# A second DMA queue for part of the expert weights: the down matrices' transfers issued by ScalarE

## The reference

```python
D_MODEL = 1024; SEQ = 256; N_EXPERTS = 16; CAPACITY_FACTOR = 2; EXPERT_FF = 2 * D_MODEL
# expert_w_gate_2, expert_w_up_2: (1, 16, 1024, 2048)   expert_w_down_2: (1, 16, 2048, 1024)
# every expert chooses capacity = 2 * 256 / 16 = 32 tokens by their affinity;
# for its 32 tokens it computes  (silu(x @ w_gate) * (x @ w_up)) @ w_down,
# and the results, scaled by the affinity, are added to those tokens' rows of h
```

## Time and profile before

| | us |
|---|---|
| median of three runs | 1963.32 (1962.98 to 1967.84) |
| the profiled execution, its own time | 1964.53 |
| its span in the trace | 1962.7 |
| busy time: TensorE matmuls | 1537.9 (78%) |
| busy time: VectorE | 622.9 (32%) |
| busy time: ScalarE | 525.6 (27%) |
| expert weight transfers issued | 192, of 2048 KB each |
| median from issue to landing, gate, up, down | 46.9, 45.9, 45.2 |

### The profile page before, as it was taken

The page is one execution under the profiler, slowest core; times in us unless marked ns, Lnnn a source line. Parts: engine busy times, 40 slices in busy tenths (PEclk is TensorE's granted clock), DMA queues, the critical chain, the costliest instruction groups (busy, mean ns, idle before and its releaser), DMA issues.

```text
span 1962.7 us, 25924 instructions
## 1 busy us (share of the span) xinstructions
PE 1537.9 (78%) x11225; PEld 1047.0 (53%) x11243; DVE 622.9 (32%) x956; ACT 525.6 (27%) x859; POOL 134.1 (7%) x151
## 2 busy tenths in 40 slices
PE   7999999999999997899898656666556666665655
PEld 7888999897999897689573211121111221111111
DVE  4565444666444544445742000000000000000000
ACT  6445343545434445435531000000000000000000
POOL 0251000030000013310200000000000000000000
PEclk9999999999999989999989877677887777778787
DMA  9443555443555444223186999999999999999997
GB/s 272 135 143 124 185 192 182 140 142 117 184 181 191 121 127 129 65 68 108 45 341 278 428 427 428 428 427 428 428 427 427 428 427 427 428 427 428 428 428 309
DMA packets 138529, 542.00 MB, mean 276 GB/s; under 512 B 10062, under 2 KB 103459, under 8 KB 113859
## 3 DMA queue, kind: packets, MB, share of 16 engines
q1 hardware_dynamic: 138386, 540.50, 70.1%
q0 software_dynamic: 48, 0.13, 0.0%
HBM read 539.56 MB, written 1.05 MB: 275 GB/s over the span
## 4 chain that ended last, share of the span: by engine, by line
PE 48%; DMA 40%; DVE 5%; ACT 3%; POOL 2%; issue 1%; SPq 0%; DVEq 0%; ACTq 0%; POOLq 0%
DMA ew<-in_expert_w_down_dram 21%; PE bank L1039 12%; PE bank L1040 11%; PE bank L1041 11%; DMA ew<-in_expert_w_up_dram 9%; DMA ew<-in_expert_w_gate_dram 9%; PE bank L1518 3%; PE bank L1534 2%; POOL arena L663 1%; PE bank L1178 1%; PE bank L1061 1%; ACT wH L706 1%; PE bank L1123 1%; PE bank L1252 1%; PE bank L1046 1%
## 5 line engine op out<-in xcount | busy, mean ns | idle before, releaser
L1518 PE MATMUL bank<-ew,xeT 128*32 128x512 f32 x2048 | 334.1, 795 | 184.1 <-DMA ew<-in_expert_w_up_dram 130.8
L1555 DVE TENSOR_TENSOR wL<-ring,wH 128x2048 fp32r<-128x2048 f32 x128 | 294.8, 2303 | 285.2 <-ACT wH L706 284.9
L706 ACT ACTIVATE wH<-ring 128x2048 fp32r<-128x2048 f32 x128 | 244.1, 1907 | 308.8 <-PE bank L1041 306.7
L1039 PE MATMUL bank<-xH,wH 128*128 128x256 f32 x1056 | 302.7, 287 | 4.4 <-DVE wL L1555 4.2
L1040 PE MATMUL bank<-xL,wH 128*128 128x256 f32 x1056 | 299.4, 284 | 0.0
L1041 PE MATMUL bank<-xH,wL 128*128 128x256 f32 x1056 | 299.4, 283 | 0.0
L1518 PEld LDWEIGHTS bank<-ew,xeT 128*32 128x32 f32 x2048 | 66.8, 132 | 435.3 <-DMA ew<-in_expert_w_up_dram 210.7
L1534 PE MATMUL bank<-ew,tok 128*32 128x256 f32 x2048 | 178.9, 511 | 100.1 <-DMA ew<-in_expert_w_down_dram 93.2
L1039 PEld LDWEIGHTS bank<-xH,wH 128*128 128x128 f32 x1056 | 203.0, 192 | 10.4 <-issue 8.1
L1040 PEld LDWEIGHTS bank<-xL,wH 128*128 128x128 f32 x1056 | 203.1, 192 | 0.8
L1041 PEld LDWEIGHTS bank<-xH,wL 128*128 128x128 f32 x1056 | 203.1, 192 | 0.0
(11 more groups left out here) (274 smaller groups left out, 1803.2 us busy)
## 6 DMA issues: line engine op xcount, KB each, us to landing
ew<-in_expert_w_gate_dram SPq DMA_DIRECT2D x64, 2048.0 KB, 46.9
ew<-in_expert_w_up_dram SPq DMA_DIRECT2D x64, 2048.0 KB, 45.9
ew<-in_expert_w_down_dram SPq DMA_DIRECT2D x64, 2048.0 KB, 45.2
ring<-in_w_gate_up_dram SPq DMA_DIRECT2D x44, 1024.0 KB, 5.1
ring<-in_w_down_dram SPq DMA_DIRECT2D x22, 1024.0 KB, 4.9
ring<-in_w_in_dram SPq DMA_DIRECT2D x22, 1024.0 KB, 5.3
ring<-in_w_out_dram SPq DMA_DIRECT2D x12, 1024.0 KB, 4.9
ring<-in_w_in_fox_dram SPq DMA_DIRECT2D x10, 1024.0 KB, 8.8
```

The costliest lines, as they stand in the source:

```text
L706: act.activation(wH[:, n % 2, w], ring[:, slot(n), w], ACT.Copy).then_inc(w_hi, 1)
L1039: pe.matmul(out, lh, rh, start=start, stop=False)
L1518: mm = pe.matmul(bank[half][32 * j:32 * j + 32, :], xeT[:, k, CAP * e:CAP * e + CAP], w_[:, m, 512 * j:512 * j + 512], start=(k == 0), sto ...
L1555: dve.tensor_tensor(wL[:, n % 2, w], ring[:, slot(n), w], wH[:, n % 2, w].bitcast(F32), ALU.subtract).then_inc(w_split, 1)
```

## The change

The function that issues one unit, `load_expert`, moves out of SyncE's block and takes the issuing engine as an argument. The first expert is left as it was. From the second expert on, SyncE leaves out units 8 to 11. ScalarE issues these four one behind the other, between its wait for the gate product (`e_used` at 12 e + 4) and its Silu. A slot's earlier unit has then been multiplied in every case, since the latest that unit 11 needs is `e_used` at 12 e + 2. The slots, the sizes and the order in which TensorE uses the units stay the same.

```diff
+        def load_expert(queue, e, u):
+            g = e * EU + u
+            if u < 8:
+                src = (e_gate, e_up)[u // 4][0, e].rearrange("(u p m) f -> u p (m f)", p=P, m=2)[u % 4]
+            else:
+                src = e_down[0, e].rearrange("(u p m) d -> u p (m d)", p=P, m=4)[u - 8]
+            queue.dma_start(ew[:, eslot(g), :], src).then_inc(e_full[eslot(g)], 16)
...
             for g in range(ESLOTS, NE * EU):
-                sp.wait_ge(e_used, g - ESLOTS + 1)
-                load_expert(g // EU, g % EU)
+                if g % EU < 8 or g < EU:
+                    sp.wait_ge(e_used, g - ESLOTS + 1)
+                    load_expert(sp, g // EU, g % EU)
...
                 act.wait_ge(e_used, e * EU + 4)
+                if e > 0:
+                    for u in range(8, EU):
+                        load_expert(act, e, u)
                 act.activation(sg, bank[0][:, :], ACT.Silu).then_inc(e_sg, 1)
```

More of the change, by code:

```diff
@@ L554, in _ @@
                 load_rows(n, w_out2[0], 2 * P * i)
[L556 to L562, removed]
             dif = att_base["dif"]
@@ L566, in _ @@
             for g in range(3):
-                load_expert(0, g)
+                load_expert(sp, 0, g)
             sp.wait_ge(w_split, NU - 4)
-            load_expert(0, 3)
+            load_expert(sp, 0, 3)
             sp.wait_ge(sn_ss, 4)
             sp.wait_ge(mTL, 4)
-            load_expert(0, 4)
+            load_expert(sp, 0, 4)
             sp.wait_ge(w_split, NU)
-            load_expert(0, 5)
-            load_expert(0, 6)
+            load_expert(sp, 0, 5)
+            load_expert(sp, 0, 6)
             sp.wait_ge(w_used, NU)
-            load_expert(0, 7)
-            load_expert(0, 8)
+            load_expert(sp, 0, 7)
+            load_expert(sp, 0, 8)
             sp.wait_ge(xe_mm, KD)
-            load_expert(0, 9)
+            load_expert(sp, 0, 9)
             for g in range(ESLOTS, NE * EU):
-                sp.wait_ge(e_used, g - ESLOTS + 1)
-                load_expert(g // EU, g % EU)
+                if g % EU < 8 or g < EU:
+                    sp.wait_ge(e_used, g - ESLOTS + 1)
+                    load_expert(sp, g // EU, g % EU)
             for q in range(4):
```

## The result

The changed kernel took 2007.97 us (median, 2006.18 to 2010.9) beside 1964.63 us of the kernel before in the same session: a ratio of 1.022, 95% interval 1.020 to 1.024. The prediction was 1969.3 us with a range from 1961 to 1988; it was wrong. The profiled execution has a span of 2009.1 us, 46.4 more than before. (Of the many executions of the kernel before that stand beside the experiments, one took 2501 us; it counts in no ratio.)

What follows compares the result with a forecast made beforehand. The prediction took the sixteen DMA engines to bound the expert stage, 58.8 us per expert. SyncE 0, Silu 0, cycle 0 and end +6 on a median of 1963.3 gave 1969.3 us, range 1961 to 1988.

Steps and rivals of the forecast that it cites:

- what bounds the kernel, and what a change could touch: Expert stage: DMA engines set the pace, 58.8 us per expert; only idle engines or work behind the last landing move time.
- Silu: ScalarE: Silu waits behind four issues, 1.3 us, at worst 11.6, but this is hidden; counted as 0.
- the order of service: DMA engines with two full queues: taken as half and half, packet by packet.
- SyncE in part: SyncE without the down units: skipping four issues per expert is worth nothing, gate units issued no earlier; counted as 0.
- The bound of 2.9 us for one issue: ScalarE's issues: 0.33 us each, up to 2.9 when the queue is full, so at worst 11.6 us for four.
- service in the order of issue: Rival on the two queues: down units land behind units issued earlier, end unchanged, +0, 1963 us; chance 0.12.
- the cycle costs nothing: Expert stage, steady state: engines never stop, since the down-unit path takes 57.5 us against the engines' 58.8; counted as 0.
- The path by the down units: From one complete gate product to the next through down-unit landings and products: 57.5 us, 1.3 us to spare.
- settles at three units of backlog: Expert cycle: about three up units outstanding at each complete gate product, unit 7 landing 29.1 us behind it.
- The forecast's median of 40 us: Down units in the steady state: median time from issue to landing falls to 40 us.
- the cycle is longer: Rival: expert cycle exceeds 58.8 us; at 61, about 1985 us; costlier half, about 2075 at share 0.4; chance 0.2.
- the end, +6: Last expert: TensorE ends 8 to 10 us after the last landing, before 3.1; 5.2 to 7 later, taken as 6.

Runs made afterwards that it cites:

- experiment 7: Changed kernel with ScalarE's Silu placed ahead of its four down-unit issues instead of behind them: 2005.99 us, ratio 1.022 to the kernel before.
- experiment 8: Changed kernel with the next expert's gate units 0 and 1 held on SyncE's queue for four more products: 1963.68 us beside 1963.56 of the kernel before.
- experiment 1: Changed kernel's late down-unit moments (e_used = 12 e + 4), but all transfers issued by SyncE on one queue: 1961.47 us beside 1965.06 of the kernel before.
- experiment 3: Changed kernel with TensorE multiplying zeros while it waits, from the second expert on, no transfer touched: 1973.56 us, ratio 1.005 to the kernel before.
- experiment 5: Changed kernel with TensorE multiplying zeros in its waits, but not between the last expert's down units: 1966.22 us beside 1963.95 of the kernel before.
- experiment 2: Changed kernel with ScalarE's four issues two gate units earlier, at e_used = 12 e + 2: 1965.12 us beside 1965.06 of the kernel before.
- experiment 9: Changed kernel with ScalarE issuing the down units near the moments of the kernel before: 1975.9 us beside 1963.56 of the kernel before.
- experiment 6: Changed kernel with ScalarE's four issues one gate unit earlier, at e_used = 12 e + 3: 1974.67 us beside 1963.56 of the kernel before.

## Why the prediction was wrong, step by step

**Right: what bounds the kernel, and what a change could touch.** Only idle engines or work behind the last landing could move the time; the whole loss is idle engines: 951.3 less 905.8 us is 45.5, against 46.4 in the span. The rest is the start of the stage, 0.9 us later.

**Right: Silu and the order of service; SyncE in part.** The four issues took 2.0 us and Silu was not on the path (experiment 7). (The bound of 2.9 us for one issue, and with it the 11.6 for four, was read from one row; the longest in the trace of before took 3.8 us, and both issues of the earlier trace rows had nine units outstanding.) SyncE issued the gate units no earlier, as forecast, but that they no longer stand behind the down units was not worth nothing: held back, they gave the whole loss back (experiment 8). Two queues share half and half (624 to 562 packets), so service in the order of issue did not occur; experiment 1 shows what it would have given, the predicted +0.

**Wrong: "the cycle costs nothing".** This is the step that failed, by the sizes of its terms; the path itself is the one that bound the kernel. The path by the down units was put at 57.5 us against 58.8. In the cycle shown above:

| term | predicted | measured |
|---|---|---|
| issue to last landing | 1.9 + 39.2 = 41.1 | 44.9 |
| last down unit's products | 1.9 | 3.7 |
| to the next gate product | 5.1 | 6.3 |
| four gate units | 9.4 | 9.8 |
| sum | 57.5 | 64.7 |

The largest miss, 3.8 us, is the latency. It was taken from output transfers of another kind at the end of the kernel, 1.9 us, where 5.7 stood: the first packet starts 3.7 us behind the first issue, the packets of the four units then take 40.2 us and not 39.2, and the landing comes 1.0 us behind the last of them. The second, 1.8 us, is the clock: the last down unit was counted at 2.4 GHz, though the forecast itself had it arrive 9.8 us behind the one before. It ran at 3.6 us in every cycle from expert 5 to 14, and experiments 3 and 5 show that the clock is enough to undo the loss: transfers as slow as in the change, and the time is back. It is not the only term that is enough; two gate units' time does it (experiment 2), and so does a sooner landing (experiment 8). The way to the gate product varied between 5.3 and 6.3 us and the gate product between 8.2 and 9.8, both by the clock (the gate product takes 7.1 in every cycle from expert 2 on in experiment 5); that gives the mean of 63.5 rather than 64.7.

**Wrong: "settles at three units of backlog".** That balance exists only if the path by the down units is shorter than 58.9 us. It was longer, so the backlog ran out. It paid for the first experts, as the rival had it: DMA share 1.01 up to 1300 us, 0.96 and 0.94 after that. The last up unit landed 29.2 us behind ScalarE's first issue in expert 1, the forecast's 29.1, then 23.5, 14.7, 9.7 and 1.5 us.

**A slip beside the sum.** The forecast's median of 40 us from issue to landing for down units does not follow from its own half rate: four units that land 9.8 us apart have a median near 25, and 24.8 was measured. Only the last one takes some 43 us from its own issue.

**The rival "the cycle is longer" was what happened**, at a chance of 0.2 and too low a price. At the measured mean from expert 5 on it gives 10 x 4.6 = 46 us; it was priced at 22 us, for a cycle of 61. The costlier half of this rival had been left outside the range.

**Wrong in the sum, though the mechanism exists: the end, +6.** With no backlog left, nothing was late behind the last landing. TensorE in the last expert of the changed kernel:

```profile
1998.57 3.23 PE L1538 MATMUL bank<-ew,tok 128*32 128x256 f32 x32 [1.87 <-DMA ew<-in_expert_w_down_dram]
```

3.2 us behind the last landing, beside 3.1 before: +0. It showed in experiment 9 instead, at +12.

**Not settled.** Experiment 8 gained more than worked out, and experiment 6 lost less; in both the second queue's packets started sooner behind their issue (1.0 to 3.4 and 1.7 to 2.1 us in the later experts). In experiment 8 the time to the last down unit's landing went from 36.8 to 44.7 us from cycle to cycle, in experiment 6 from 42.7 to 45.1; no run separates what of that is the other queue's backlog and what is the late start itself.

## What to carry to other kernels

When a transfer is issued behind a product that itself waits for that transfer's predecessors, look for the closed cycle from one issue to the next, add it up with cold-clock durations and the latency seen beside a busy queue, and hold it against what the engines need per round; within a few per cent of it, don't count the cover as given. Here the two queues shared by halves and not by need: what is needed first did well ahead in one queue (experiment 1), or with less beside it (experiment 8). A digit of nine tenths hides a loss of 5%; read the rate.

## What was not expected of the hardware

- In the change the second queue's first packet started 3.4 to 4.2 us behind its issue when the other queue had work, although from expert 6 on that work had been issued at most 1.7 us earlier, and 1.0 us when it had none. Work in the other queue is not the whole of it: in experiment 2 it was 1.0 us in the last two experts too, with two of SyncE's units still 14 and 16 us from landing. What sets it is not shown.
- Two full queues moved 429 GB/s, as one did (428): no gain and no loss by the interleaving.
- A down unit took TensorE 1.9 us or 3.6 us, by the clock level; 74 products of zeros per expert in the waits raised the granted clock from 0.66 to 0.91 and were worth 40 us here, while 26 in the kernel before were worth nothing.
